# Half of h gathered in place of the normed rows, the norm's factors applied later, and half of h added to each expert result

## The reference, cut to what matters

```
h = h + merged @ w_out                      # 1024 real tokens, D = 1024
u = rmsnorm(h, ffn_norm)                    # h * rsqrt(mean(h^2) + eps) * ffn_norm
# top group of 8, in it the top 2 of 8 experts, gates gate_1 and gate_2
h = h + sum_k gate_k * ((silu(u @ w1[e_k]) * (u @ w3[e_k])) @ w2[e_k])
out = rmsnorm(h, final_norm)
```

## Time and profile before

| | us |
|---|---|
| median of 3 runs | 1476.52 (1475.53 to 1476.92) |
| the profiled execution | 1478.93 |
| its span, first to last instruction | 1477.2 |
| TensorE busy | 1377.7 (93%) |
| VectorE busy | 583.8 (40%) |
| ScalarE busy | 565.3 (38%) |
| GpSimd busy | 101.7 (7%) |

### The profile page before, as it was taken

How to read it: one execution, slowest core, us unless ns; L and a number is a source line. 1 busy time by engine, 2 the same in 40 slices (tenths; PEclk the granted TensorE clock), 3 DMA queues, 4 the chain that set the end, 5 groups by cost and what they waited for, 6 DMA issues and landing times. The chain is left out here.

```text
span 1477.2 us, 21003 instructions
## 1 busy us (share of the span) xinstructions
PE 1377.7 (93%) x8447; PEld 978.8 (66%) x8447; DVE 583.8 (40%) x1306; ACT 565.3 (38%) x1066; POOL 101.7 (7%) x131
## 2 busy tenths in 40 slices
PE   5999999999999999999989999999997888798887
PEld 5887888788888877677768888855544444344442
DVE  5555555433441154657768556411110111111117
ACT  6535354322322247545553455433332222223223
POOL 0000000000000000000000011211111111111100
PEclk9999999999999999989999999999999999999999
DMA  6111111112234334112137745999999999999998
GB/s 187 43 30 36 37 30 43 30 33 72 85 100 114 97 85 142 61 37 72 44 116 245 283 165 170 328 417 419 419 419 420 419 420 419 419 420 420 418 400 351
DMA packets 122242, 312.53 MB, mean 212 GB/s; under 512 B 31121, under 2 KB 77201, under 8 KB 96801
## 3 DMA queue, kind: packets, MB, share of 16 engines
q1 hardware_dynamic: 110112, 285.96, 51.5%
q0 software_dynamic: 12032, 25.22, 4.4%
HBM read 283.81 MB, written 41.98 MB: 221 GB/s over the span
## 5 line engine op out<-in xcount | busy, mean ns | idle before, releaser
L2411 PE MATMUL ps<-r,m_xT 128*64 128x256 f32 x2048 | 258.9, 406 | 59.3 <-DMA r<-in_w 59.0
L130 PE MATMUL ps<-uTh,h_wh 128*128 128x512 f32 (+2 forms) x672 | 256.1, 381 | 4.4 <-DVE uTl L567 2.4
L131 PE MATMUL ps<-uTl,h_wh 128*128 128x512 f32 (+2 forms) x672 | 248.4, 370 | 0.0
L132 PE MATMUL ps<-uTh,h_wl 128*128 128x512 f32 (+2 forms) x672 | 248.1, 369 | 0.0
L2411 PEld LDWEIGHTS ps<-r,m_xT 128*64 128x64 f32 x2048 | 145.8, 140 | 153.3 <-DMA r<-in_w 65.9
L2327 DVE TENSOR_TENSOR m_prod<-m_sig,ps 128x128 f32<-128x128 f32 x64 | 18.4, 288 | 329.4 <-ACT m_sig L2298 325.6
L130 PEld LDWEIGHTS ps<-uTh,h_wh 128*128 128x128 f32 x672 | 126.9, 189 | 27.5 <-DVE uTl L567 4.3
L132 PEld LDWEIGHTS ps<-uTh,h_wl 128*128 128x128 f32 x672 | 126.9, 189 | 18.9
L131 PEld LDWEIGHTS ps<-uTl,h_wh 128*128 128x128 f32 x672 | 127.1, 189 | 18.3 <-issue 0.2
L2393 PE MATMUL ps<-r,m_hT 128*64 128x512 f32 x512 | 122.3, 598 | 1.3 <-DVE m_hT L2331 0.9
L2288 ACT ACTIVATE m_y<-ps,gate 64x512 f32<-64x512 f32 x128 | 87.3, 682 | 80.1 <-PE ps L2393 78.4
(11 more groups left out here) (369 smaller groups left out, 2131.5 us busy)
## 6 DMA issues: line engine op xcount, KB each, us to landing
r<-in_w SPq DMA_DIRECT2D x190, 1024.0 KB
h_w<-in_w_in SPq DMA_DIRECT2D x37, 512.0 KB, 4.2
gates<-h_sg POOLq DMA_DIRECT2D x16, 512.0 KB, 2.9
r<-y_moe SPq DMA_DIRECT2D x8, 1024.0 KB, 16.1
br_gate<-gates SPq DMA_DIRECT2D x14, 512.0 KB, 4.5
e_wo<-in_w_out SPq DMA_DIRECT2D x4, 1024.0 KB, 7.4
f_x<-in_x SPq DMA_DIRECT2D x8, 512.0 KB, 4.8
h_mid<-f_x SPq DMA_DIRECT2D x8, 512.0 KB, 4.5
```

The costliest lines, as they stand in the source:

```text
L130: pe.matmul(out, lh, rh, start=start, stop=False)
L131: pe.matmul(out, lh, rl, start=False, stop=False)
L132: return pe.matmul(out, ll, rh, start=False, stop=stop)
L2411: ins = pe.matmul(bank(UP_BANK + e % 2, 0, DE, CAP * f, CAP * (f + 1)).rearrange("p (r f) -> p r f", r=2), xT[i % 2][:, j, CAP * k:CAP * ( ...
```

## The change

Only h/2 goes to HBM (`h_half`), once a tile; `u_moe` and its stores are gone. The experts gather rows of h/2. The norm's gain is applied where the turned rows leave PSUM (`turned_rows`, now on VectorE, with a gain of one number a partition and column group), and the norm's factor of each token, doubled, is applied in the two products on VectorE and in the sigmoid on ScalarE; it reaches them as a fourth list, `scale`. Each token has two result rows, so half of h is added to each before it is scattered: on GpSimd for 31 pairs, on VectorE for the last. The tail then loads no h.

```
@@ output_part, gpsimd
-            pool.wait_ge(u_out, 16 * TT)
+            pool.wait_ge(half_out, 16 * TT)
...
@@ output_part, scalar: valued
                 for k in range(2):
-                    act.activation(one[:, k, 1, :], one[:, k, 2, :], ACT.Copy, scale=g.rec[:, t, k, 1:2]).then_inc(Vg_ok, 1)
+                    act.activation(one[:, k, 1, :], one[:, k, 3, :], ACT.Copy, scale=g.rec[:, t, k, 1:2]).then_inc(Vg_ok, 1)
+                    act.activation(one[:, k, 2, :], one[:, k, 3, :], ACT.Copy, scale=g.rec[:, t, k, 3:4]).then_inc(Vg_ok, 1)
@@ output_part, vector
+            def halved(t, q):
+                cols = slice(q * 512, (q + 1) * 512)
+                if t:
+                    dve.wait_ge(half_out, 16 * t)
+                dve.wait_ge(h_ok, 2 * t + q + 1)
+                dve.tensor_scalar(half[:, cols], x[t % 2][:, cols], 0.5, None, ALU.mult).then_inc(half_ok, 1)
@@ vector: shared
+                for k in range(2):
+                    c.mark(dve.tensor_scalar(g.rec[:, t, k, 3:4], sc[:, 14:15], 2.0, None, ALU.mult))
@@ tensor: lists
-                pe.matmul(LISTS(0, 3 * EXPERTS), Pm[:, 1, :], V[t % 2][:, 1, :, :].rearrange("p v e -> p (v e)"),
+                pe.matmul(LISTS(0, 4 * EXPERTS), Pm[:, 1, :], V[t % 2][:, 1, :, :].rearrange("p v e -> p (v e)"),
...
@@ experts_part, sync: the tail
             for t in range(TT):
                 load_y(t)
-                if t + 2 < TT:
-                    load_h(t + 2)
@@ experts_part, gpsimd
             for i in range(PAIRS):
+                if i == LAST:
+                    pool.wait_ge(dn_mm, EXPERTS - NBUF + 2)
+                    pool.iota(token, pattern=[[1, SEQ]], base=0, channel_multiplier=0,
+                              allow_small_or_imprecise_dtypes=True).then_inc(io_ok, 1)
+                if i >= 1:
+                    n = i - 1
+                    pool.wait_ge(y_ok, 4 * n + 4)
+                    pool.tensor_tensor(y[n % XB][:, :], y[n % XB][:, :], x[n % XB], ALU.add).then_inc(added_ok, 1)
+                    pool.wait_ge(added_ok, n + 1)
+                    settle(pool, g)
+                    pool.indirect_dma_start(out=g.y, out_offset=bass.IndirectOffsetOnAxis(ap=g.dst[:, n:n + 1], axis=0),
+                                            in_=y[n % XB][:, :], in_offset=None,
+                                            bounds_check=2 * SEQ - 1, oob_is_err=False).then_inc(y_out[n % XB], 16)
                 n = i + XB - 1
                 if n < PAIRS:
                     if n >= XB:
...
-                    pool.indirect_dma_start(out=x[n % XB], out_offset=None, in_=g.u2,
+                    pool.indirect_dma_start(out=x[n % XB], out_offset=None, in_=g.h,
...
-                if i == LAST:
...
-                if i >= 1:
-                    n = i - 1
-                    pool.wait_ge(y_ok, 4 * n + 4)
-                    settle(pool, g)
-                    pool.indirect_dma_start(out=g.y, out_offset=bass.IndirectOffsetOnAxis(ap=g.dst[:, n:n + 1], axis=0),
...
@@ experts_part, vector
+            def turned_rows(i):
...
+                for q in range(2):
...
+                    dve.tensor_tensor(xT[i % 2][:, 4 * q:4 * q + 4, :], bank(X_BANK + q).rearrange("p (j t) -> p j t", j=4),
+                                      by_gain(q, P), ALU.mult).then_inc(xT_ok, 1)
...
+            dve.wait_ge(y_ok, 2 * EXPERTS)
+            dve.tensor_tensor(y[LAST % XB][:, :], y[LAST % XB][:, :], x[LAST % XB], ALU.add).then_inc(last_added, 1)
...
-                dve.tensor_tensor(h[t], h[t], g.ps[:, added(t):added(t) + D], ALU.add).then_inc(sum_ok, 1)
+                dve.tensor_tensor(total[t], pair[t][:, 0, :], g.ps[:, added(t):added(t) + D], ALU.add).then_inc(sum_ok, 1)
                 if t:
                     scaled(t - 1)
-                if 2 <= t + 1 < TT:
-                    first(t + 1)
```

More of the change, by code:

```diff
@@ L1612, in output_part @@
         sb = lambda n, s, d=F32: here.enter_context(nc.sbuf_tensor(n, s, d))
-        gain, hT = g.norm_gain, g.hT
-        u, junk = sb("f_u", [P, D]), sb("f_junk", [P, 512])
+        half, hT = g.half, g.hT
+        junk = sb("f_junk", [P, 512])
         R = GROUPS + EXPERTS
@@ L1654, in load_x, with store @@
                 sp.dma_start(x[t % 2][:, :], g.x[0, t * P:(t + 1) * P, :]).then_inc(x_in[t % 2], 16)
[L1656 to L1662, removed]
+            def store(t):
+                sp.wait_ge(half_ok, 2 * t + 2)
+                sp.dma_start(g.h[t * P:(t + 1) * P, :], half[:, :]).then_inc(half_out, 16)
             with nc.allow_non_contiguous_dma(reason="a small gain turned once"):
@@ L1704, in sync @@
             sp.wait_ge(w_mm, 2 * TT)
-            store_u(TT - 1)
+            store(TT - 1)
             g.load_down(sp, 4, 4)
             g.load_down(sp, 5, 5)
-            store_h(TT - 1)
             sp.wait_ge(g.x_in[0], 16)
@@ L1957, in vector @@
                 else:
-                    gained(0)
+                    halved(t, 0)
                 add(t, 1)
@@ L2251, in late @@
                 settle(pool, g)
-                pool.indirect_dma_start(out=late_x, out_offset=None, in_=g.u2,
+                pool.wait_ge(last_added, 1)
+                pool.indirect_dma_start(out=late_x, out_offset=None, in_=g.h,
                                         in_offset=bass.IndirectOffsetOnAxis(ap=late_rows[:, 2:3], axis=0),
@@ L2304, in late @@
             def late(k, e, c):
-                for q in range(2):
-                    act.wait_ge(v_x_tr, 2 * k + q + 1)
-                    act.activation(late_xT[:, 4 * q:4 * q + 4, :], turned(X_BANK + q, 4), ACT.Copy).then_inc(v_xT_ok, 1)
+                act.wait_ge(last_added, 1)
                 act.wait_ge(v_up_mm, k + 1)
-                act.activation(late_sig[:, :], late_bank(UP_BANK, 0, DE, CAP), ACT.Sigmoid).then_inc(v_sig_ok, 1)
+                act.activation(late_sig[:, :], late_bank(UP_BANK, 0, DE, CAP), ACT.Sigmoid,
+                               scale=late_scale[:, :]).then_inc(v_sig_ok, 1)
                 act.wait_ge(v_h_tr, k + 1)
@@ L2324, in vector @@
         def vector(dve):
+            by_gain = lambda q, n: g.gain_t[:, 4 * q:4 * q + 4].rearrange("p (j a) -> p j a", a=1).to_broadcast([P, 4, n])
+            def turned_rows(i):
+                if i:
+                    dve.wait_ge(x_tr, i + 1)
+                if i >= 2:
+                    dve.wait_ge(up_mm, 2 * (i - 2) + 2)
+                for q in range(2):
+                    if i == 0 and q == 0:
+                        dve.wait_ge(x_half, 1)
+                    elif i == 0:
+                        dve.wait_ge(x_tr, 1)
+                    dve.tensor_tensor(xT[i % 2][:, 4 * q:4 * q + 4, :], bank(X_BANK + q).rearrange("p (j t) -> p j t", j=4),
+                                      by_gain(q, P), ALU.mult).then_inc(xT_ok, 1)
+            turned_rows(0)
             for e in range(EXPERTS):
                 dve.wait_ge(sig_ok, e + 1)
-                dve.tensor_tensor(prod[:, :], sig[e % 2][:, :], bank(UP_BANK + e % 2, 0, HALF), ALU.mult).then_inc(prod_ok, 1)
+                dve.scalar_tensor_tensor(out=prod[:, :], in0=bank(UP_BANK + e % 2, 0, HALF), scalar=g.scale[:, e:e + 1],
+                                         in1=sig[e % 2][:, :], op0=ALU.mult, op1=ALU.mult).then_inc(prod_ok, 1)
                 dve.wait_ge(prod_ok, e + 1)
-                dve.tensor_tensor(hid[:, :], prod[:, :], bank(UP_BANK + e % 2, HALF, HALF), ALU.mult).then_inc(hid_ok, 1)
+                dve.scalar_tensor_tensor(out=hid[:, :], in0=bank(UP_BANK + e % 2, HALF, HALF), scalar=g.scale[:, e:e + 1],
+                                         in1=prod[:, :], op0=ALU.mult, op1=ALU.mult).then_inc(hid_ok, 1)
+                if e % 2 == 0 and e // 2 + 1 < PAIRS:
+                    turned_rows(e // 2 + 1)
                 dve.wait_ge(h_tr, e + 1)
```

142 lines of the change are left out of this document (53 added, 89 removed).

## The result

The changed kernel takes 1653.99 us (median of 4 runs, 1648.56 to 1655.66) against 1476.03 us before (4 runs, 1475.08 to 1476.92). The ratio is 1.1204, with a 95% interval of 1.1187 to 1.122: slower by 178 us. The forecast was 1595 us, 118 us slower, with a range up to 1644.

The account below looks back on a forecast made before the run. Transfers set the mean pace of 15.28 us a pair; a new loop through GpSimd would make it 19.4. Span 1477.2 + 119.5 + 1.8 - 2.5 = 1596 us, forecast time 1595 us, range 1522 to 1644.

Parts of the forecast that it names:

- the loop: Experts: turn, down product, results, addition, scatter, gather, landing, next turn; 18.9 us, with clock 19.4 a pair against 15.28.
- the clock term of the loop: TensorE falling to the slow clock while it waits for gathered rows: 0.5 us a pair, bounds 0 and 1.7.
- the landing of 9.6: Gathered rows arriving after the gather's issue on GpSimd: 9.6 us in each pair, plus 0.3 for TensorE to start.
- Results' end: From the start of a turn to the end of the pair's results, down product included: 4.40 us.
- The addition: GpSimd's addition of 128x1024 to a pair's results: 2.3 us, bounds 1.0 to 2.6; then 0.85 us to the scatter.
- Scatter to gather: On GpSimd, from the scatter's issue to the next gather's issue: 1.31 us.
- MEMSET, head: MEMSET ahead of the last gather: 1.8 us more; routing and first gather before the experts: together nothing, within 1 us.
- The tail: Output part after the experts: last sum 2.0 us earlier, with the experts' end 2.5 us less in all.
- Waits for weights: TensorE's waits for weight loads in the experts: nearly gone in the changed profile.
- The gather did not land sooner: Rival: thinned weight loads let gathers land in 6.8 us, loop 16.06 us, time 1498 us; chance 0.12.
- The rival with the clock falling at every wait: Loop with slow clock, addition 3.2 us and landing 11: 22.2 us a pair, 1676 us; chance 0.14.

Follow-up runs that it names:

- the run with 52: Changed kernel with 52 small unneeded matmuls ahead of each turn from pair 3 on, to keep TensorE busy while it waits: 1740.22 us, ratio 1.1801.
- the run with 24: Changed kernel with 24 small unneeded matmuls as filler ahead of each turn from pair 3 on: 1618.07 us, ratio 1.0972.
- the runs with the gather first: Changed kernel with the gather issued ahead of the scatter: 1557.89 us; also with the addition on VectorE: 1525.97; or with four gathered-row tiles, two result tiles: 1476.09.
- four tiles: Changed kernel with four tiles for gathered rows and two for results, in place of three and three: 1476.32 us, ratio 1.0005.
- two runs: Changed kernel without GpSimd's addition: 1599.61 us; kernel before with only the scatter of pair n-3 moved ahead of the gather of pair n: 1594.48 us.
- the run without w3: Changed kernel with the loads of w3 left out from expert 7 on, stale w3 used: 1633.0 us, one run.

## Why the prediction was wrong in size and right in mechanism

The loss is there, in the loop and at the place that the prediction gave. With the mean pace of a pair its sum closes: 29 x (21.30 - 15.28) = 174.6 us, and 1.2 us less between the last turn and the last sum, are 173.4 us; the spans differ by 1650.7 - 1477.2 = 173.5. The step that failed is the clock term of the loop, "I take 0.5, bounds 0 and 1.7", and behind it, smaller, the landing of 9.6. Point by point:

- **Results' end.** Forecast 4.40 us after the turn's start, 4.50 to the addition, and 0.5 for the clock: 5.0. Measured 6.40. At full clock it is 4.44 (the run with 52) to 4.77 (the run with 24), so the 4.50 was right and the clock 1.6 to 2.0 us, about its upper bound of 1.7. The prediction's own argument said that a fall costs nothing in the idle time. That is true, and was the wrong question: what costs is the return, and it comes with the first work after the wait, which is always the turn. The bound came from one up product of the earlier trace rows that was partly slow, and I should have taken it whole. Beyond the forecast this is 1.4 us a pair, 41 us of the 55 by which the span exceeds the sum of 1596.
- **The addition.** Forecast 2.3 us and 0.85: measured 2.38 (2.37 to 2.40) and 0.86. The half of the page's figure for 2048 columns in the Trainium skill, "GPSIMD Engine Reference", section 3.1, 2.25 us, was 5% short.
- **Scatter to gather.** 1.31 us, measured 1.29 to 1.35.
- **The landing.** Forecast 9.6 us and 0.3: measured 10.31 from gather to turn, 0.41 us a pair or 12 us. The forecast put less than full engines into the price (86% of the loop). The gathers of the earlier trace rows flew with full engines and behind a scatter, as these do, and their median of 10.4 would have been the price. The scatter ahead is about 2 us of it (the runs with the gather first), so the forecast's reason, the engines' load alone, was not the whole one.
- **MEMSET, head.** Turn 2 stands at 967.76 us in the timeline, where it stood at 967.70, so nothing came of the head, as forecast, but by luck. The last lists product did not start 0.5 us later but 0.7 us sooner (941.83 against 942.50), turn 0 followed the first gather's issue by 5.9 us and not 6.9, and stood 1.5 us sooner (950.03 against 951.53). By 958 us the lead was gone: ScalarE's table load of 1.28 us, which stood at 953.36 beside the first up product, now stands at 955.43, behind that product and ahead of the first sigmoid, and TensorE waited 1.57 us for what follows from it. The prediction has no term for this. The MEMSET lies within the mean above.
- **The tail.** Forecast 55.4 us from the last turn to the last sum, measured 56.7: the last steps of the experts have part of the slow clock too (the last down product takes 3.10 us, and took 1.94). With four tiles the last sum came 1.6 us earlier than before, of 2.0 forecast for it.
- **Waits for weights.** Forecast nearly gone; the up product waited 0.4 us in all, and that for the turned rows. A first fast stretch isn't there, as said: turn 3 stands at 987.72.
- **The rivals.** The gather did not land sooner: the median is 10.3 us, with only the last one, alone, at 3.7. The Trainium skill's figure in "DMA: Bandwidth & Descriptors", section "Anatomy of one DMA", 3.2 us by the estimate, is 0.5 us short of that last one and far from every other. The rival with the clock falling at every wait had the fall right (it gave it 1.0 us, in place of 1.6 to 2.0), but its addition of 3.2 us and its landing of 11 did not come. Its 22.2 us a pair lay nearer to the measured 21.30 than the forecast's 19.4, but by two terms that did not come.

What is shown: that the loop is the whole cause (four tiles), that order and addition share it two to one (two runs), that the clock is worth 36 us of it (filler), and that the scatter ahead of the gather costs 1.9 us beyond its issue. (These prices overlap, since the clock and the landing lie in the loop that the order closes; they are not to be added up.) What stays open is how the engines share their time between GpSimd's transfers and SyncE's loads: that a gather is slow because it flies within a burst of loads rests on the stretches and on the last gather, the run without w3 supports it only weakly, and no run issued a gather alone in mid-stream.

## What to carry to other kernels

When a change ties a buffer's release to later work, draw the loop that now closes and sum it; if it exceeds the pace of the bound, each microsecond in it is paid once a round. Taken out again, 1.2 to 2.2 us of it gave back 0.6 to 0.8 of themselves here, since the landing grew. Price what lies in the loop as it is there and not in the mean: the engine that waits comes back at the slow clock, and the transfer that is waited for flies just when the work before it has released the big loads, here behind another transfer too. One more buffer was worth 178 us here, exchanging two instructions 96 us; and where neither engine nor transfer was on the loop, the same exchange was worth nothing.

## What was not expected of the hardware

- A scatter of 0.5 MB issued 1.3 us ahead of a gather made the gather's median landing 10.3 us in place of 8.3 (three tiles), and 10.9 in place of 8.1 with four tiles, where the engines were full either way (share 1.02). The scatter issued second lost as much: 10.4 in place of 8.4, and 10.1 in place of 8.1.
- VectorE's scaling and GpSimd's addition, each reading two operands in SBUF, slowed each other: 1.28 to 2.07 us and 2.35 to 3.34 us. The Trainium skill, "SBUF — State Buffer", section "SBUF: two separate sides", says that the two engines share a pair of ports as an exclusive lock held for a whole instruction. The trace agrees in the main: a scaling that started at 1450.42 us, 0.63 us behind an addition, took 2.81 us while that addition kept its 2.36, and the next addition took 3.18. But the tiles follow each other at 3.3 us, less than 1.28 + 2.35 = 3.63, so some 0.3 us of the two did overlap. VectorE's sums, with one operand in PSUM, kept their 1.21 us beside the additions, and in the loop of the experts the addition kept its 2.38 us.
- After some 6.5 us without work the granted clock was 0.50, and the eight transposes behind it took 1.94 us in place of 1.09.
